# Norms, gates and bonus of a recurrence moved from a stage of their own into the recurrence's next period

## What is computed

```python
# DeltaNet heads: o comes from the chunked recurrence
o = rmsnorm(o, norm_w) * silu(z)
# RWKV heads: y comes from the recurrence
mean = mean(y); var = mean(square(y - mean))
y = (y - mean) * rsqrt(var + 64e-5) * ln_w + ln_b
bonus = sum(r_h * k_h * r_k) * v_h
y = (y + bonus) * g            # g = sigmoid(gd) @ g2
mix = concatenate([o, y]) @ ab_w_out
h = h + rmsnorm(mix, norm_mix_post[0])
```

## Time and profile before

| what | us |
|---|---|
| runs shown (3) | 1621.16 median, 1619.26 to 1625.39 |
| the profiled execution | 1617.55, of which the span is 1615.5 |
| input projection ends (last L324) | 232.25 |
| recurrence, four periods | 233 to 426.8 |
| `recur` of tile 3 | 426.8 to 437.2 |
| norms and gates, up to the first product of the output projection | 437.2 to 481.0 |
| PE busy | 92% of the span, at a mean granted clock of 0.968 of full speed |

### The profile page before, as it was taken

One profiled execution on the slowest core, in us unless ns is written; L12 is line 12 of the kernel. 1 busy time (PEld: TensorE's weight loads), 2 busy tenths in 40 slices (PEclk: granted clock), 3 DMA queues, 4 the chain that ended last, 5 costly groups with the idle time before them and its releaser, 6 DMA issues.

```text
span 1615.5 us, 24865 instructions
## 1 busy us (share of the span) xinstructions
PE 1493.2 (92%) x9841; PEld 1243.7 (77%) x9841; DVE 848.1 (53%) x1395; ACT 667.6 (41%) x1145; POOL 93.6 (6%) x132
## 2 busy tenths in 40 slices
PE   6999987999829999999999996799979999999997
PEld 4776766888628988888888884698868988888886
DVE  4367537666485554324526426588765443334433
ACT  5533413443534443224425325567665433124321
POOL 0100003221150000000000000100000000000000
PEclk9999999999959999999999997799999999999999
DMA  5222200000123333223322421100021233323321
GB/s 218 77 78 79 79 0 1 2 2 2 48 78 123 109 100 117 92 79 97 106 85 81 128 79 62 43 2 2 2 94 59 98 92 118 92 79 103 106 90 53
DMA packets 32605, 119.36 MB, mean 74 GB/s; under 512 B 3696, under 2 KB 3824, under 8 KB 32496
## 3 DMA queue, kind: packets, MB, share of 16 engines
q1 hardware_dynamic: 29808, 108.84, 21.2%
q10 hardware_dynamic: 2688, 8.98, 1.5%
HBM read 115.71 MB, written 2.10 MB: 73 GB/s over the span
## 4 chain that ended last, share of the span: by engine, by line
PE 63%; DVE 5%; ACT 1%; issue 1%; ACTq 0%; DVEq 0%
PE bank L322 18%; PE bank L323 18%; PE bank L324 18%; PE bank L2241 2%; PE bank L2254 2%; PE bank L2230 1%; PE bank L2231 1%; PE bank L2081 1%; DVE nmax L2311 1%; PE bank L2232 1%; DVE wl_m L315 0%; PE bank L2137 0%; PE bank L2118 0%; PE bank L2059 0%; DVE ul_m L444 0%
## 5 line engine op out<-in xcount | busy, mean ns | idle before, releaser
L315 DVE TENSOR_TENSOR wl_m<-ring,wh_m 128x1024 fp32r<-128x1024 f32 x144 | 176.5, 1225 | 183.2 <-ACT wh_m L307 180.7
L307 ACT ACTIVATE wh_m<-ring 128x1024 fp32r<-128x1024 f32 x144 | 152.8, 1061 | 216.6 <-PE bank L324 207.2
L322 PE MATMUL bank<-uh_m,wh_m 128*128 128x512 f32 (+2 forms) x576 | 213.9, 371 | 3.9 <-DVE ul_m L444 2.1
L323 PE MATMUL bank<-ul_m,wh_m 128*128 128x512 f32 (+2 forms) x576 | 213.3, 370 | 0.0
L324 PE MATMUL bank<-uh_m,wl_m 128*128 128x512 f32 (+2 forms) x576 | 213.3, 370 | 0.0
L322 PE MATMUL bank<-wh_m,hh 128*128 128x512 f32 x448 | 174.4, 389 | 0.0
L323 PE MATMUL bank<-wl_m,hh 128*128 128x512 f32 x448 | 174.3, 389 | 0.0
L324 PE MATMUL bank<-wh_m,hl 128*128 128x512 f32 x448 | 174.3, 389 | 0.0
L1765 DVE TENSOR_TENSOR hraw<-hraw 128x512 f32<-128x512 f32 x64 | 44.3, 692 | 159.0 <-ACT hraw L1721 158.9
L322 PEld LDWEIGHTS bank<-uh_m,wh_m 128*128 128x128 f32 x576 | 108.4, 188 | 22.9 <-DVE ul_m L444 2.9
L1721 ACT ACTIVATE hraw<-bank 128x512 f32<-128x512 f32 x64 | 38.4, 600 | 207.3 <-PE bank L324 206.8
(11 more groups left out here) (410 smaller groups left out, 2773.5 us busy)
## 6 DMA issues: line engine op xcount, KB each, us to landing
ring<-in_wstream_dram SPq DMA_DIRECT2D x200, 512.0 KB, 3.5
rowbuf<-in_rows_dram ACTq DMA_DIRECT2D x6, 512.0 KB, 4.5
xres<-in_x_dram SPq DMA_DIRECT2D x4, 512.0 KB, 6.7
xres<-in_x_dram ACTq DMA_DIRECT2D x1, 2048.0 KB, 7.8
out_dram<-xres ACTq DMA_DIRECT2D x4, 512.0 KB, 4.0
prerow<-in_rows_dram ACTq DMA_DIRECT2D x3, 512.0 KB, 4.9
con<-in_consts_dram SPq DMA_DIRECT2D x1, 869.5 KB, 13.4
par<-in_params_dram SPq DMA_DIRECT2D x1, 680.5 KB, 11.8
```

The lines of the kernel that those rows point to most:

```text
L307: a.sig(a.e.activation(dn[2][:, c % RING, :], slot(c), ACT.Copy), sem("w_hi"), it * per + c + 1)
L315: v.sig(v.e.tensor_tensor(dn[3][:, c % RING, :], slot(c), dn[2][:, c % RING, :].bitcast(F32), ALU.subtract), sem("w_lo"), it * per + c + 1)
L322: pe.matmul(out, lh, rh, start=start, stop=False)
L323: pe.matmul(out, lh, rl, start=False, stop=False)
```

## The change

Per tile, the steps of the old stage are put into the streams of the next period; the stage with its two barriers is gone. What is left for tile 3 stands between the recurrence and the output projection or inside the latter.

- PE: `gate_product` of tile k-1 after `level_y` 1 of period k (tile 3: after `level_y` 3 of period 3). `turn_o` 0 stands inside `recur` 3, `turn_o` 1 and 2 behind it, `turn_o` 3 in the output projection before chunk 36. The projection waits for `o_low` 3, the low parts of tiles 0 to 2.
- DVE: `y` is no longer copied but summed (L1515) and centred (L1516) in `recur`. `gate_parts`, `square_sums` and `weighted` of tile k-1 stand in period k, `finished` 0 to 2 before `recur` 3.
- ACT: `z` is evicted with Silu at the end of the input projection, all four tiles on ACT (two were DVE's). `squares` of tile k-1 in period k, `roots` of three tiles in period 3 and of the last behind `recur` 3.
- POOL: the bonus of tile k-1 between levels 2 and 3 of period k, the gate of `o` behind level 6, the scaling of `o` at the end.
- `SC` is swapped (ring for even tiles), so that the ring is free after tile 2 and the stream waits for three tiles only. Buffers are laid out anew (`exn`, `Xb`, `U`, `gB`, `Ds` and others in another order); `o_n`, `y_n` and `t1` are gone.

```diff
-            sp.wait_ge(sem("yr_ready"), NT)
+            sp.wait_ge(sem("yr_ready"), NT - 1)
...
-        SC = [... for x in (xres, ring)]
+        SC = [... for x in (ring, xres)]
...
             used(e, N_IN0)
-            for i in range(1, NT, 2):
-                e.activation(z[:, i, :], bank[Z_BANK[i]][:, :], ACT.Copy)
+            for i in range(NT):
+                e.activation(z[:, i, :], bank[Z_BANK[i]][:, :], ACT.Silu)
...
+            def bonuses(m):          # POOL
...
+                g.link(e.tensor_tensor(heads8(b_of(m)), heads8(fT[:, VRB:VRB + 4, tcol(m)]), w, ALU.mult))
+                g.sig(e.tensor_tensor(b_of(m), b_of(m), rowbuf[:, 512:1024]..., ALU.add), sem("by_pool"), 1 + m + 1)
+            def gated(m):            # POOL
...
+                g.link(e.tensor_tensor(o_of(m), o_of(m), z[:, m, :]..., ALU.mult))
+            def scaled_o(m):         # POOL
+                e.wait_ge(sem("inv_norm"), 3 + m // 3)
+                g.sig(e.tensor_tensor(o_of(m), o_of(m), hst[:, 1, m, 0:GH]..., ALU.mult), sem("by_pool"), 5 + m + 1)
...
+            def turn_o(m):           # PE
+                pe.wait_ge(sem("m_sb"), m + 1)
+                pe.wait_ge(sem("by_pool"), 5 + m + 1)
+                if m == 2:
+                    pe.wait_ge(sem("o_low"), 1)
...
                 if m:
                     pe.wait_ge(sem("o1_sb"), m)
+                if last:
+                    turn_o(0)
                 for h in range(GH):
                     ins = pe.matmul(bank[4]..., Dn[:, m % 2, h, :], VN[:, h, :], start=True, stop=True)
...
+            split_o(0)               # ACT, behind recur(3)
+            high_o(a, 0)
+            split_o(1)
+            high_o(a, 1)
+            squares(NT - 1)
+            e.dma_start(xres[:, :, :], x_d).then_inc(sem("aux_loaded"), 16)
+            pre_in(e, 1, prerow)
+            high_o(a, 2)
+            roots(2, slice(3, 4))
+            split_o(2)
+            split_o(3)
+            e.wait_ge(sem("normed"), 12 + NT)
+            row_in(e, 0)
+            high_o(a, 3)
+            for k in range(4, KD):
+                split_o(k)
...
+            def gate_parts(m):       # DVE
...
+                v.link(e.tensor_tensor(A, b4(2), rowbuf[:, 0:512]..., ALU.mult))
+                v.sig(e.tensor_tensor(b_of(m), b4(2), b_of(m), ALU.mult), sem("normed"), 12 + m + 1)
+            def square_sums(m):
...
+            def weighted(m):
+                v.link(e.tensor_tensor(y_of(m), y_of(m), A, ALU.mult))
+            def finished(m):
+                v.link(e.tensor_tensor(heads8(y_of(m)), heads8(y_of(m)), per_head(4, m), ALU.mult))
+                v.sig(e.tensor_tensor(y_of(m), y_of(m), b_of(m), ALU.add), sem("m_sb"), m + 1)
...
-                e.tensor_copy(fT[:, RB:RB + 4, tcol(m)], b4(5)).then_inc(sem("y_done"), 1)
+                v.link(e.tensor_reduce(hst[:, 2, m, :]..., y, AX.X, ALU.add))
+                e.scalar_tensor_tensor(heads8(y_of(m)), per_head(2, m), -1.0 / 64, y, ALU.mult, ALU.add).then_inc(sem("y_done"), 1)
...
                 level_t(k, 2)
+                if k:
+                    gate_parts(k - 1)
                 level_x(k, 3)
...
                 level_t(k, 4)
+                if k:
+                    square_sums(k - 1)
...
                 level_x(k, 5)
+                if k:
+                    weighted(k - 1)
                 if ahead:
                     scores(k + 1, 3)
+                else:
+                    gate_parts(k)
                 level_t(k, 5)
...
+            inverses(1, slice(0, 3))
             corrected(NT - 1)
+            for m in range(NT - 1):
+                finished(m)
             recur(NT - 1)
+            split_o(0)               # DVE: here the low part of chunk 32
+            low_o(v, 0)
+            low_o(v, 1)
+            split_o(1)
+            square_sums(NT - 1)
+            weighted(NT - 1)
+            low_o(v, 2)
+            inverses(2, slice(3, 4))
+            finished(NT - 1)
+            split_o(2)
+            split_o(3)
+            low_o(v, 3)
+            for k in range(4, KD):
+                split_o(k)
...
+            if n == 0:               # PE, output projection
+                pe.wait_ge(sem("o_low"), 3)
             for k in range(KD):
+                if n == 0 and k == 4:
+                    turn_o(3)
                 weights(pe, first + k)
```

More of the change, by code:

```diff
@@ L1069, in turn_t, with gate_product @@
                     ins.then_inc(sem("tt_turned"), 1)
+            def gate_product(m):
+                if m == NT - 1:
+                    pe.wait_ge(sem("normed"), 12 + m)
+                pe.matmul(bank[2][:, :], fT[:, GD, tcol(m)], PR("g2"), start=True, stop=True).then_inc(sem("g_ready"), 1)
+            def turn_o(m):
[3 more added lines that the diff above has]
+                    pe.wait_ge(sem("o_low"), 1)
+                for x, b in ((o_of(m), OB[m]), (y_of(m), OB[m] + 1)):
+                    for q in range(4):
+                        ins = pe.transpose(bank[b][:, q * P:(q + 1) * P], x[:, q, :], ident)
+                ins.then_inc(sem("turned"), 1)
             def recur(m):
@@ L1129, in recur @@
                     ins.then_inc(sem("p_ready"), 1)
+                if last:
+                    turn_o(1)
+                    turn_o(2)
             pe.wait_ge(sem("state_init"), 1)
@@ L1151, in chunk_pe @@
                 level_y(k, 1)
+                if k:
+                    gate_product(k - 1)
                 if ahead:
@@ L1164, in chunk_pe @@
                     scores(k + 1, 1)
+                else:
+                    gate_product(k)
                 level_x(k, 4)
@@ L1181, in chunk_pe, with high_o, low_o, turned_o @@
             recur(NT - 1)
+            return turn_o
+        OB = (0, 2, 0, 6)
+        def high_o(a, m):
+            a.e.wait_ge(sem("turned"), 8 + m + 1)
+            for h in range(2):
+                hi, _, src = turned_o(m, h)
+                a.sig(a.e.activation(hi, src, ACT.Copy, scale=PR("gnorm") if h == 0 else 1.0), sem("high_done"), 8 + 2 * m + h + 1)
+        def low_o(v, m):
+            for h in range(2):
+                v.e.wait_ge(sem("high_done"), 8 + 2 * m + h + 1)
+                hi, lo, src = turned_o(m, h)
+                ins = v.e.scalar_tensor_tensor(lo, src, PR("gnorm") if h == 0 else 1.0, hi.bitcast(F32), ALU.mult, ALU.subtract)
+                v.link(ins) if h == 0 else v.sig(ins, sem("o_low"), m + 1)
+        def turned_o(m, h):
+            w = (slice(None), slice(4 * h, 4 * h + 4), tok(m))
+            return DM[0][w], DM[1][w], b4(OB[m] + h)
         def chunk_act(a):
             e = a.e
+            e.dma_start(rowbuf[:, :], rows[4:5, :].to_broadcast([P, D])).then_inc(sem("aux_loaded"), 16)
+            def squares(m):
+                e.wait_ge(sem("o_done"), m + 1)
+                a.sig(e.activation(o_squares(m), o_of(m), ACT.Square), sem("sq_done"), 12 + 2 * m + 1)
+                e.wait_ge(sem("y_done"), m + 1)
+                a.sig(e.activation(y_squares(m), y_of(m), ACT.Square), sem("sq_done"), 12 + 2 * m + 2)
+            def roots(n, tiles):
+                e.wait_ge(sem("ss_sb"), n)
+                a.link(e.activation(hst[:, 0, tiles, 0:GH], hst[:, 0, tiles, 0:GH], ACT.Sqrt, bias=eps, scale=1.0 / P))
+                a.sig(e.activation(hst[:, 3, tiles, :], hst[:, 3, tiles, :], ACT.Sqrt, bias=ln_eps, scale=1.0 / 64), sem("root"), 2 + n)
             def exps(n):
@@ L1268, in chunk_act @@
                     keys(k + 1)
-                for lv in (3, 4, 5):
-                    level_u(k, lv)
+                level_u(k, 3)
+                if k:
+                    squares(k - 1)
+                level_u(k, 4)
+                level_u(k, 5)
                 if ahead:
@@ L1585, in oproj_dve @@
             e = v.e
-            for k in range(KD):
-                split_lo(v, [None, None] + list(o_weights(first + k, first)), first + k)
+            if n:
+                for k in range(KD):
+                    split_lo(v, [None, None] + list(o_weights(first + k, first)), first + k)
             if n == 0:
```

253 lines of the change are left out of this document (107 added, 146 removed).

## The result

The changed kernel takes 1634.67 us (median of 6 runs, 1630.34 to 1635.76), the kernel before 1621.24 beside it: a ratio of 1.0072, with a 95% interval of 1.0053 to 1.0092. It is slower by 0.7%, where 1609 was forecast and the range ended at 1617. The profiled execution took 1635.76, with a span of 1633.5 and a mean granted clock of 0.957.

A forecast was written before the change was run, and what follows sets the result against it. PE, busy 92%, was taken as the bound, idling most in the norms-and-gates stage that DVE paces. 32.0 - 10.9 - 1.0 - 5.0 - 1.8 - 1.0 = 12.3 gained, from 1621.2 to 1609; range 1600 to 1617.

The forecast's parts named there:

- 32.0 for the start of the projection: Output projection starts at 448.95 instead of 480.99, 32.0 us gained if the recurrence took no longer.
- 1.0 for the Silus: End of the input projection: four Silus on ACT end after 2.2 instead of 1.1, costing 1.0 us.
- 5.0 for chunk 36: Inside the output projection: turns of 1.0 and then 4.0 of idle PE before chunk 36, costing 5.0 us.
- 1.8 for the clock behind it: Output projection: the new gap of 4.0 should bring one spell at half clock, costing 1.8 us.
- The periods without the clock: Recurrence: work moved into periods 1, 2 and 3 costs 3.6 + 3.8 + 3.5 = 10.9 us.
- the 1.3 of the sum and the centring: DVE in `recur`: sum and centring replace the copy of `y`; 1.3 with POOL's bonus beside, all passing in period 3.
- What was costed at nothing: Recurrence: POOL's bonuses and gates, ACT's squares, and ACT's roots with their table load fit into existing waits, costing nothing.
- 1.0 for both: Periods 1 and 2: clock loss behind the grown gaps before the turns, 0 to 1.9 each, taken as 1.0 together.
- rival (e): Recurrence: PE's clock does not come back, making the kernel slower than before; 36 us at half gives 1625; 4%.
- (a): The forecast itself, 1609 with its own range of 1604 to 1613; gain bounded by 15 and 10; 62%.
- the longer table load: ACT's roots before `TT`: with a drain of about 1.38 us behind the load, the gain would be 1.3 smaller.
- Rival (b): Recurrence: DVE's insertions find room as other waits shrink, only 1.5 of period 3 remaining there; 24 gained, 1597; 10%.

The follow-up runs named there:

- third run: The changed kernel with VectorE's inserted work in another order, such as sums of squares and weighting behind the last scores in periods 1 and 2: 1614.13 us, 0.9956.
- tenth run: The kernel before with `wl_m` alone moved by 384 bytes and everything behind it by 512, no instruction changed: 1631.05 us, 1.0064.
- fifth run: The kernel before with three more VectorE additions on dead data ahead of the scores of level 4 in periods 1 and 2: 1632.81 us, 1.0058.
- run two: The changed kernel with the free stretch ahead of `uh_m` cut from 4480 to 4096 bytes, no instruction changed: 1621.17 us, 0.9998.

## Why the prediction was wrong

**Right:**

- *32.0 for the start of the projection.* 32.3 measured. PE's gap behind `recur` 3, forecast to shrink from 43.8 to about 12, is 10.7 (467.46 to 478.14).
- *1.0 for the Silus.* 0.8.
- *5.0 for chunk 36 and 1.8 for the clock behind it.* 1.03 for the turns, 3.82 of wait, and 1.7 more for the eleven steps behind it (4.22, seven of them at 0.43 instead of 0.23). Taking the wait away gave back 5.0 on PE's timeline. But "PE stands idle so long" needn't be: ScalarE and VectorE wait 14.3 and 10.6 us for the turns, and it takes one number to use that.
- *The periods without the clock,* 10.9. 10.5 measured (25.9 less 15.4), in part by parts that cancel. The wait for the scores grew by 2.17, where 2.2 was written, to 2.64. The wait for the products grew by 0.87, where 1.4 was; period 3 waits 2.89 for `Xb` 1, 1.97 more than before, where the 1.3 of the sum and the centring was written, and 1.06 more ahead of the last levels, where 1.6 to 1.7 was. These waits grew by 9.1, other idle time shrank by 2.4, and PE's gate products, written as 0.5 that a wait of 0.58 hides, are two a tile and 0.96, 3.8 in all.
- *What was costed at nothing.* With VectorE reordered PE's waits for the products and the scores are the 0.58 and 0.47 of before, so POOL's bonuses and gates and ScalarE's squares are indeed covered. The roots with their table load are too: `TT` waits for PE as before. The drain that the Trainium skill (ScalarE: Activation LUTs, What ACT_TABLE_LOAD costs) adds to a load would have made ScalarE late by 1.3, by the forecast's count; the trace shows 1.51 of waiting for PE before that `TT`, and the first root 0.02 behind the load's end (451.40 and 1.28, then 452.70).

**Wrong, step one: the clock.** "Anything from 0 to 1.9 each; I take 1.0 for both", and nothing at all for period 3. The rows held a gap of 2.64 with the clock at half behind it, and my forecast was 2.9 for two gaps of the new kernel. A gap like the one known to do it should have been charged in full. The wait ahead of `level_y` 1 in period 3, by my own terms 0.92 and 1.3, lay between the 2.06 that had done nothing and the 2.64, and got no charge; it came to 2.89. The size of a spell was wrong too. I had taken it from a stage of long products, and the spells in the recurrence are longer: four with 36 us at half, one of them behind a wait of 1.40, which the rows gave no reason to charge. The clock took 15.4 of the 25.9 by which the periods grew, where the sum had 1.0. That is rival (e), which had 4%: "it decides if gaps of 2 to 3 us recur in one period"; it named 36 us for 1625. Its price of 0.45 for a microsecond was near what was measured, 0.42 in the third run and 0.43 here (15.4 over 36).

**Wrong, step two: a part of the diff without a term.** The free stretch ahead of `uh_m` was read as bookkeeping. It costs 12 us in the changed kernel (1.0072 to 0.9998) and 16 in the one before (12 between the two profiles), through some 2000 products that the change doesn't touch, at 6 ns each. With the 1.7 behind chunk 36 that is nearly all of the 14.9 in the last row of the table. No row of the trace before could have priced it; but "buffers are laid out anew" could have stood among the unknowns, with a bound. Without it the kernel stands at 1621, outside the range still, by the clock alone: 1609 and 14.0, by which the periods missed, are 1623.

**Slips in the sums.** They don't decide anything. The lower bound of (a)'s gain is 12.3, less 2.8 for two full spells (3.8 in place of 1.0), less 1.3 for the longer table load: 8.2 and not 10. Rival (b) leaves out the 1.8 for the clock behind chunk 36 and should read 22.7 gained. And the stage before holds eight gate products, not four; the earlier trace rows shows five of them. The gap before the turns, written as 2.9, is 2.67 by its own terms (0.47 and 2.2).

**And a sentence that went too far:** in periods 1 and 2 "DVE is already the late one at the places where new DVE work is put", from which it seemed to follow that all of it passes. VectorE is late there, and free three instructions later: PE has the turns and a `level_y`, some 3 us, in hand behind the scores. The insertions cost 0.22 a period there (third run: a wait of 0.22 for `Ti`). Rival (b), 1597, came out for another place in the same period.

## What to carry to other kernels

Work moved into a full stage should stand behind, not ahead of, what the bounding engine waits for: 3.5 us of VectorE work in each of two periods cost most of 19 us in one place and 0.2 a period a few instructions further on. Charge a new wait on TensorE at more than its length when the profile has one of that size with the clock at half behind it; here waits that grew by 9 us drew some 15 with them. And when buffers are laid out anew, compare the mean of the costliest product groups far from the change; a few nanoseconds in some thousand products are one per cent of the kernel.

## What the runs showed of the hardware

Three things I had not expected. A product of 128x512 starts on average 226 to 227 ns after the one before it when the operands of the sequence lie a multiple of 512 bytes apart, and in the groups of 448 that were slow 231 to 236 when they don't; remainders of 32 and 64 already cost it. The Trainium skill (TensorE: Matmul & The Clock Gate, Step-by-step: what each phase is for) says that loading the next tile's weights takes no SBUF read bandwidth from the running matmul; by that the place of `wl_m` could not matter to `ul_m` with `wh_m`, and the tenth run has 396 ns in place of 389. The measurement decides. One wait of 2.64 to 2.9 us can be followed by anything from 3 to 17 us at half clock, though TensorE is busy from its end on. And twice, in the fifth run and in the tenth, the clock fell in the recurrence for 20 us without any long wait; where the tenth has it, the five other kernels with the same instructions have it full. Shorter waits go both ways: the 2.06 of the earlier trace rows, without effect there, has the clock at half behind it in two of the twelve profiles (run two, 0.72 over 262 to 268, and run ten, 0.66 over 259 to 264). Why is open.
